# Three transformer layers on one core: the delta rule's inverses are built in five interruptions in place of seven and used four steps sooner, and the first searched block's rounds are put later on VectorE

## What is computed

```python
# gated delta rule, 4 heads, chunks of 64 tokens in the reference
lmat = jnp.where(strict, jnp.einsum('nbhid,nbhjd->nbhij', k_beta, kc) * decay, 0.0)
tmat = lax.linalg.triangular_solve(eye + lmat, eye, left_side=True, lower=True, unit_diagonal=True)
u = jnp.einsum('nbhij,nbhjd->nbhid', tmat, v_beta)
w = jnp.einsum('nbhij,nbhjd->nbhid', tmat, k_beta * jnp.exp(gc)[..., None])
# recurrence over the chunks
v_new = u_i - w_i @ state
o = (q_i * exp(g_i)) @ state + a_i @ v_new
state = state * exp(g_last) + (k_i * exp(g_last - g_i)).T @ v_new

# sparse attention: for each query the 128 best keys by a score
score = jnp.einsum('bqh,bqhs->bqs', wi_b, jax.nn.relu(dots))
_, idx = lax.top_k(jnp.where(causal, score, -inf), topk)
```

## Time and profile before

| what | us |
|---|---|
| median of 3 runs | 1945.31 |
| lowest and highest | 1943.90, 1945.67 |
| the profiled execution, its own time | 1945.25 |
| its span in the trace | 1943.4 |

### The profile page before, as it was taken

The page is one execution under the profiler, slowest core; times in us unless marked ns, Lnnn a source line. Parts: engine busy times, 40 slices in busy tenths (PEclk is TensorE's granted clock), DMA queues, the critical chain, the costliest instruction groups (busy, mean ns, idle before and its releaser), DMA issues.

```text
span 1943.4 us, 23699 instructions
## 1 busy us (share of the span) xinstructions
PE 1927.1 (99%) x9082; PEld 1532.2 (79%) x9082; DVE 1028.3 (53%) x1842; ACT 891.3 (46%) x1361; POOL 851.7 (44%) x646
## 2 busy tenths in 40 slices
PE   9999999999999999999999999999999999999999
PEld 6878887877788878787877888677766788888887
DVE  6667755555745678666365657575644435101210
ACT  6455553344345565543343355586555344312321
POOL 5545432433355454423334445455222445444443
PEclk9999999999999999999999999999999999999999
DMA  5334542423534235632414545322111332222232
GB/s 201 128 119 134 138 133 80 153 82 119 192 111 162 87 116 156 156 105 71 153 65 143 191 151 162 136 77 97 66 55 55 120 109 87 99 96 98 97 114 71
DMA packets 94559, 227.61 MB, mean 117 GB/s; under 512 B 29968, under 2 KB 33040, under 8 KB 93136
## 3 DMA queue, kind: packets, MB, share of 16 engines
q1 hardware_dynamic: 88752, 222.95, 34.8%
q10 hardware_dynamic: 5696, 3.15, 0.7%
HBM read 193.95 MB, written 24.64 MB: 112 GB/s over the span
## 4 chain that ended last, share of the span: by engine, by line
PE 85%; DVE 8%; ACT 2%; DMA 2%; SPq 1%; issue 1%; POOL 1%; ACTq 0%; DVEq 0%
PE bank L444 83%; DVE kv L378 1%; DVE ER L378 1%; PE bank L448 1%; SPq L373 1%; DMA X<-inverses 1%; DVE scs L403 1%; DMA kv<-blocks 1%; DVE tmp L378 1%; DVE m8s L400 0%; ACT lt L430 0%; DVE lt L388 0%; DVE tmp L388 0%; ACT L422 0%; ACT wh L433 0%
## 5 line engine op out<-in xcount | busy, mean ns | idle before, releaser
L378 POOL TENSOR_TENSOR wl<-st,wh 128x512 fp32r<-128x512 f32 x602 | 802.7, 1356 | 1016.1 <-ACT wh L433 1016.1
L444 PE MATMUL bank<-hh,wh 128*128 128x512 f32 x1616 | 651.5, 404 | 2.0 <-DVE hl L388 0.6
L444 PE MATMUL bank<-hh,wl 128*128 128x512 f32 x1616 | 629.6, 390 | 0.0
L444 PE MATMUL bank<-hl,wh 128*128 128x512 f32 x1616 | 629.2, 390 | 0.0
L433 ACT ACTIVATE wh<-st 128x1024 fp32r<-128x1024 f32 (+1 forms) x302 | 316.9, 1050 | 236.9 <-PE bank L444 189.1
L444 PEld LDWEIGHTS bank<-hh,wh 128*128 128x128 f32 x1616 | 303.5, 188 | 88.9 <-issue 24.1
L444 PEld LDWEIGHTS bank<-hl,wh 128*128 128x128 f32 x1616 | 303.8, 188 | 66.7 <-issue 6.9
L444 PEld LDWEIGHTS bank<-hh,wl 128*128 128x128 f32 x1616 | 303.4, 188 | 64.5
L378 DVE TENSOR_TENSOR xt<-xt,bank 128x512 f32<-128x512 f32 x40 | 27.4, 687 | 235.6 <-PE bank L444 235.6
L430 ACT ACTIVATE tmp<-bank 128x512 f32<-128x512 f32 x70 | 41.7, 596 | 157.8 <-PE bank L444 151.0
L444 PE MATMUL bank<-fh,wl 128*128 128x512 f32 x256 | 99.7, 389 | 0.0
(11 more groups left out here) (353 smaller groups left out, 2844.7 us busy)
## 6 DMA issues: line engine op xcount, KB each, us to landing
st<-units SPq DMA_DIRECT2D x300, 512.0 KB, 3.5
gates<-tmp SPq DMA_DIRECT2D x48, 256.0 KB, 2.8
gt<-gates SPq DMA_DIRECT2D x48, 256.0 KB, 3.7
pads<-tmp SPq DMA_DIRECT2D x32, 128.0 KB, 2.7
qk<-tmp SPq DMA_DIRECT2D x16, 256.0 KB, 4.2
x_scratch<-xt SPq DMA_DIRECT2D x2, 2048.0 KB, 9.2
xt<-x_scratch SPq DMA_DIRECT2D x2, 2048.0 KB, 8.8
ph<-phi SPq DMA_DIRECT2D x8, 512.0 KB, 4.7
```

The source lines that it names most:

```text
L378: return NOTHING if self.e is None else self.e.tensor_tensor(out, a, b, op)
L444: return NOTHING if self.e is None else self.e.matmul(out, lhsT, rhs, start=start, stop=stop, skip_group_check=share)
```

## The change

- `INVERSE, BACK` go from (21, 11) to (17, 9): the steps between the last of the four heads' blocks and the first W product are 17 in place of 21, and so the W products, everything of the heads after them and the recurrence stand four steps sooner on PE, VectorE and ACT.
- `CUTS` goes from seven interruptions to five, none of them before j = 4: the substitution runs in longer pieces, and begins at the same step.
- `HELD` moves the first searched block's 16 rounds 12 steps of `select` later on VectorE, and takes 12 idle steps from the block after it, so that from the second block's scores on nothing of `select` is moved. On PE and ACT it moves nothing.
- On SP the transfer `X<-inverses` stands two steps sooner behind `inverses<-kv`; on ACT the transposed copy and its two transfers stand sooner by three and four steps. No instruction is added or removed.

```diff
-INVERSE, BACK = 21, 11
+INVERSE, BACK = 17, 9
-CUTS = (4, 8, 11, 14, 17, 21, 25)
-SELECT = (8, 12, 3)
+CUTS = (4, 10, 15, 20, 25)
+SELECT, HELD = (8, 12, 3), 12
...
# ScalarE, delta
-            yield from idle(INVERSE - BACK + 6)
+            yield from idle(INVERSE - BACK + 5)
...
-            yield from idle(BACK - 8)
+            yield from idle(BACK - 7)
...
# VectorE, select
-                yield from idle(SELECT[b - 1])
+                yield from idle(SELECT[b - 1] - (HELD if b == 2 else 0))
...
+                if b == 1:
+                    yield from idle(HELD)
...
# SyncE, delta
-            yield from idle(INVERSE - BACK + 2)
+            yield from idle(INVERSE - BACK + 4)
...
-            yield from idle(3)
+            yield
```

## The result

The changed kernel takes **1960.28 us** (median of 4 runs, 1957.10 to 1964.62), beside 1945.49 for the kernel before in the same session. The ratio is 1.0074, with a 95% interval of 1.0060 to 1.0087: 14.8 us slower. I had forecast 1950.4 and a range up to 1956.5. The direction was right, the size was not, and the time lies outside the range.

A forecast was written before the change was run, and what follows sets the result against it. PE, busy 99% of the span, was taken to bound the kernel. From 1945.25 us, +2.0 for the moved recurrence, +3.1 net for waits on the inverses and 0 for the rounds gave 1950.4, range 1941.5 to 1956.5.

The forecast's parts named there:

- VectorE and SP: First layer: substitution ends at 217.1, 13 us sooner; SP issues the inverses behind the `qk` store at 220.6.
- The trip of the inverses: Inverses stored, then loaded as X0: loads issued from 225.6, landing 4.5 after the last issue, at 232.1; W stands 1.7.
- Bank 6: Second wait, at the next half unit's transposes: bank free at 238.3; with W's standing 2.7 us first layer, 3.8 second.
- The recurrence: Moved between half units: 17.7 us against 16.72, costing 1.0 us a layer, 2 in all.
- The chain of scores: Two score pairs at the recurrence's end, through relu and sums to the stream: 4.6 us, no shorter without its filling.
- The rounds: First block's 16 rounds, moved later on VectorE beside the heads' products: hidden, cost 0; 1 us apiece if uncovered.
- (a): Rival: the inverses are in time, no wait left at W or the transposes: 1944 us (1941.5 to 1946.5); chance 0.25.
- (b): Rival: faster, below 1941.4, inverses in time and both score pairs together under 2.5 us: 1940; chance 0.12.
- (c): Rival: VectorE stays late through GpSimd's full exclusion, substitution ends at 222, W stands 5 us more each layer: 1959; chance 0.11.

The follow-up runs named there:

- The second profiled execution: The changed kernel profiled again with no edit: one execution of 1955.38 us, span 1953.5.
- the fastest version: Changed kernel with W two steps later, third block's scores four steps sooner, VectorE's operations for the first two heads two steps sooner: 1940.56 us, ratio 0.9968.
- the rounds alone: Kernel before with only the first searched block's 16 rounds 12 select steps later on VectorE: 1942.46 us, ratio 0.9979.
- with the five slices: Kernel before with the rounds 12 steps later and the substitution in five slices, begun at the same step: 1942.39 us, ratio 0.9981.
- with the scores: Kernel before with the rounds 12 steps later and the third block's scores two steps sooner: 1942.06 us, ratio 0.9974.

## Why the prediction was right or wrong

**VectorE and SP: right.** The substitution ended at 216.19, which is 216.75 on the clock of the trace before (forecast 217.1). VectorE's timeline, with the wait for the swapped halves and the emptying of bank 6:

```profile
216.02 0.17 DVE L378 TENSOR_TENSOR kv<-kv,ER 128x16 f32<-128x16 f32 x1
...
236.91 0.75 DVE L388 SCALAR_TENSOR_TENSOR tmp<-tmp,col,tabs 128x512 f32<-128x512 f32 x1 [4.01 <-DMA pads<-tmp]
...
238.84 0.68 DVE L378 TENSOR_TENSOR lT<-bank,gcol 128x512 f32<-128x512 f32 x1
```

The inverses went out behind `qk` at 220.48, or 221.0 (220.6), so the `qk` store did hold them up. SP's issues (start, us of issuing):

```profile
219.00 0.33 SPq L373 DMA_DIRECT2D qk<-tmp  x1
...
220.48 3.30 SPq L373 DMA_DIRECT2D inverses<-kv  x2
...
227.63 1.92 SPq L373 DMA_DIRECT2D X<-inverses  x4
...
230.61 1.14 SPq L373 DMA_DIRECT2D pads<-tmp  x2
```

**The trip of the inverses: right in sum, by two errors.** X was issued at 228.2 on that clock, not at 225.6: the two stores took 3.30 to issue and 5.6 to land, in place of 1.63 and 3.9. The loads then landed in 2.2, not in the 4.5 that I had put in the middle. W began at 231.97, forecast 232.1. KB and median us to landing, from 215 to 240 us:

```profile
inverses<-kv SPq DMA_DIRECT2D x2, 128.0 KB, 5.6
...
X<-inverses SPq DMA_DIRECT2D x4, 64.0 KB, 2.2
pads<-tmp SPq DMA_DIRECT2D x2, 128.0 KB, 5.1
```

**Bank 6: the mechanism right, the term too small.** I had 238.3 for the bank free, and 2.7 us for both standings in the first layer. It was 240.1, and 1.58 + 2.84 = 4.4. The swapped halves were there at 237.5, not at 235.5, as they too took 5.1 to land, where I had put 4.0. In the second layer it was 1.74 + 3.13 = 4.9 in place of 3.8. Net of before, the term was +5.2 and not +3.1.

**The recurrence: net right, split unexamined.** Forecast +1.0 a layer, measured +0.75 at full clock. The chain of scores took 5.07 from its first pair to the stream, of which 0.48 is slow clock: so 4.59 beside the 4.6 of the forecast. What I did not see is that the loss was all in that chain, and that a small shift of the scores turns the same move into a gain of 2.2 a layer.

**The step that failed: the clock behind a standing was put at nothing.** In "2.7 us in the first layer together, 3.8 in the second" and in the scores' chain of 4.6 I counted each standing by its own length and let TensorE go on at full pace behind it, without a reason. Nothing in the trace of before warned of it, as its longest bracket of 1.6 us left the clock at full. But the forecast itself put a standing of 1.7 and another close behind it, then 0.9 and a wait for the scores, where the kernel before had nothing of the kind. The half clock cost 8.9 of the 11 us by which the profiled execution (1961.45) lies above the 1950.4; the undersized standings are 2.1 more, and the recurrence took 0.5 back. Without the half clock that execution would have come to about 1952.6, inside the range. The second profiled execution, which lost 4.4 us by the clock, took 1955.38 and lies inside it as it is.

**The rounds: no cost, as forecast, but a gain that I missed.** I priced them at 0. By themselves they take the whole of the wait for the inverses away (2.6 us of standing), which I had booked under the substitution and then spent on moving W.

**The rivals.** (a) fell by both waits: 1.58 and 1.74 at W, 2.84 and 3.13 at bank 6. (b)'s condition, two pairs in under 2.5 us, was far off: 5.07. (c) gave 1959 (its own terms, 5 us in each layer on 1950.4, make 1960.4), close to the time, for a reason that is not there: VectorE was not late, and an operation that met GpSimd grew by 1.0, as in the earlier trace rows. Its closeness is chance.

## What to carry to other kernels

Price a wait on a busy TensorE twice: its length, and what the matmuls behind it lose if the clock falls (here 0 to 3.2 us behind a standing of 1.6 to 3.1, not the same from one execution to the next). When work on one engine is moved sooner, look at what stands *ahead* of the operation that frees its bank in the other engine's queue, and move that operation too. See that the tail keeps its alternation, since two products on the same bank pair, one behind the other, expose their whole chain. And split a combined change before judging it: here the part that gained 3 us was hidden under one that lost 18.

## What the runs showed of the hardware that I had not expected

Behind a wait of 1.56 us at the scores, itself 3 us behind a shorter one of 0.8, the granted clock fell to 0.50 and cost up to 3.2 us; behind 3.10 us at bank 6 it once stayed at 1.00. So the longest single standing did not tell whether the clock falls. The spread of a kernel's times goes with it: 1957.1 to 1964.6 for the changed kernel, with four such places, and 1940.2 to 1941.8 for the fastest version, whose mean granted clock was 1.000 in all six executions, where the changed kernel's was 0.994 to 0.997.

The kernel before loses the clock too, though its profiled execution did not. Of its 73 executions beside the experiments, 50 had a mean granted clock of 1.000 (median 1945.3) and 23 had 0.999 or 0.998 (median 1948.1). Between its `nr,cst` and W products 0.9 and 2.5 us are standing. Of the versions without a standing at W or at bank 6 (the rounds alone, with the five slices, with the scores, and the fastest) none of 34 executions was under 1.000. That the clock falls behind W in those 23 is an inference, as none of them was profiled.
